# Row loads, row stores and stores of the normed tiles issued from GpSimd's queue in the last mixing stage of a hybrid encoder layer

## The reference

```
h = rms_norm(x, norm1);  p = h @ w_in
y_a = gated unit on 128-position blocks of (u, v)          # group A
o, S = gated_delta_chunked(q, k, v, g, beta, S0, 64)       # group B, a recurrence over the tiles
x = x + concat(y_a, y_b) @ w_o                             # 1024 x 1024
h2 = rms_norm(x, norm2)
x = x + (silu(h2 @ w_gate) * (h2 @ w_up)) @ w_down         # d_ff = 2816
y = rms_norm(x, final_norm)
```

## Time and profile before

| | us |
|---|---|
| median of 3 runs | 2823.54 (2820.58 to 2824.5) |
| the profiled execution | 2825.7 |
| its span | 2824.0 |
| PE busy in the span | 2730.2 (97%) |
| last mixing stage with its drain, about | 900 to 1181 |

### The profile page before, as it was taken

The page is one execution under the profiler, slowest core; times in us unless marked ns, Lnnn a source line. Parts: engine busy times, 40 slices in busy tenths (PEclk is TensorE's granted clock), DMA queues, the critical chain, the costliest instruction groups (busy, mean ns, idle before and its releaser), DMA issues.

```text
span 2824.0 us, 46417 instructions
## 1 busy us (share of the span) xinstructions
PE 2730.2 (97%) x19256; PEld 2415.0 (86%) x19256; DVE 1408.1 (50%) x2303; ACT 986.1 (35%) x1634; POOL 21.6 (1%) x60
## 2 busy tenths in 40 slices
PE   8999999999999998699999999999999999999998
PEld 7877777777777776599999999999999998999998
DVE  4666667767666565534333345333434345344344
ACT  3436556655555554411111214122111134222222
POOL 2000000000000000000000000000000000000000
PEclk9999999999999999899999999999999999999999
DMA  9355444444544856532122225212222152222220
GB/s 298 96 165 175 124 124 150 137 123 124 173 123 124 155 174 226 186 112 60 59 60 74 59 66 192 70 60 59 74 59 59 67 172 75 75 74 74 74 74 37
DMA packets 361901, 315.13 MB, mean 112 GB/s; under 512 B 15653, under 2 KB 315762, under 8 KB 359714
## 3 DMA queue, kind: packets, MB, share of 16 engines
q1 hardware_dynamic: 361762, 313.20, 37.1%
HBM read 254.80 MB, written 58.36 MB: 111 GB/s over the span
## 4 chain that ended last, share of the span: by engine, by line
PE 56%; DVE 1%; ACT 1%; issue 0%; DVEq 0%; POOL 0%; ACTq 0%; POOLq 0%
PE gate_ps L2586 7%; PE gate_ps L2588 7%; PE gate_ps L2587 7%; PE up_ps L2588 6%; PE up_ps L2587 6%; PE up_ps L2586 6%; PE down_ps L2587 6%; PE down_ps L2588 6%; PE down_ps L2586 6%; DVE w_in_sb L2580 0%; ACT h_hi L2382 0%; ACT w_hi L2363 0%; DVE w_in_sb L2481 0%; DVE h_lo L2503 0%; DVE w_in_sb L2525 0%
## 5 line engine op out<-in xcount | busy, mean ns | idle before, releaser
L1640 PE MATMUL pr_p<-hT_hi_p,w_hi_p 128*128 128x512 f32 x992 | 424.9, 428 | 10.9 <-DVE hT_lo_p L1081 8.9
L1641 PE MATMUL pr_p<-hT_lo_p,w_hi_p 128*128 128x512 f32 x992 | 392.9, 396 | 0.0
L1642 PE MATMUL pr_p<-hT_hi_p,w_lo_p 128*128 128x512 f32 x992 | 392.8, 396 | 0.0
L2467 DVE TENSOR_TENSOR w_in_sb<-up_ps,w_in_sb 128x384 f32<-128x384 f32 (+1 forms) x132 | 70.7, 536 | 604.6 <-PE up_ps L2588 604.6
L2586 PE MATMUL gate_ps<-h_hi,w_hi 128*128 128x384 f32 (+1 forms) x1056 | 345.9, 328 | 17.2 <-DVE w_lo L2457 14.4
L2587 PE MATMUL gate_ps<-h_lo,w_hi 128*128 128x384 f32 (+1 forms) x1056 | 345.4, 327 | 0.0
L2588 PE MATMUL gate_ps<-h_hi,w_lo 128*128 128x384 f32 (+1 forms) x1056 | 345.3, 327 | 0.0
L2586 PE MATMUL up_ps<-h_hi,w_hi 128*128 128x384 f32 (+1 forms) x1056 | 344.0, 326 | 0.0
L2587 PE MATMUL up_ps<-h_lo,w_hi 128*128 128x384 f32 (+1 forms) x1056 | 343.9, 326 | 0.0
L2588 PE MATMUL up_ps<-h_hi,w_lo 128*128 128x384 f32 (+1 forms) x1056 | 343.9, 326 | 0.0
L2481 DVE TENSOR_TENSOR w_in_sb<-down_ps,w_in_sb 128x1024 f32<-128x1024 f32 x187 | 228.8, 1223 | 183.1 <-PE down_ps L2588 182.2
(11 more groups left out here) (378 smaller groups left out, 4063.4 us busy)
## 6 DMA issues: line engine op xcount, KB each, us to landing
w_in_sb<-in_w_in SPq DMA_DIRECT2D x100, 512.0 KB, 4.4
w_in_sb<-in_w_gate SPq DMA_DIRECT2D x66, 512.0 KB, 4.0
w_in_sb<-in_w_up SPq DMA_DIRECT2D x66, 512.0 KB, 5.2
w_in_sb<-in_w_down SPq DMA_DIRECT2D x33, 1024.0 KB, 4.9
stream_tiles<-w_in_sb SPq DMA_DIRECT2D x96, 256.0 KB, 2.5
w_in_sb<-stream_tiles SPq DMA_DIRECT2D x16, 1280.0 KB, 7.1
w_in_sb<-mixed_tiles SPq DMA_DIRECT2D x29, 512.0 KB, 5.0
out<-w_in_sb SPq DMA_DIRECT2D x21, 512.0 KB, 4.0
```

Source lines behind the costliest of these rows:

```text
L1640: pe.matmul(out, w_h, x_h, start=start, stop=False)
L1641: pe.matmul(out, w_h, x_l, start=False, stop=False)
L1642: return pe.matmul(out, w_l, x_h, start=False, stop=stop)
L2467: dve.tensor_tensor(act[:, h, 0:half], up_ps[h][:, 0:half], gate_act[:, h, 0:half], ALU.mult)\
```

## The change

The three helpers `load_rows`, `store_rows` and `store_h2` go from SP's list to POOL's, with the waits and semaphores that they had. On SP the calls of them in `quarter` fall away; nothing else of SP's list is touched. On POOL they stand behind the last `memset` in one loop over the items: load of n, both stores of the normed tile n-3, store of n-1. These are 84 transfers of 256 KB (12 loads and 12 stores of first items; 24 loads, 12 stores and 24 stores of normed halves of second items).

```
@@ SP, quarter(n, part)
                 if part == 0:
                     load_weights(n + 3)
                     if n in (ITEMS - NI + 1, ITEMS + 1):
                         load_wo(0 if n < ITEMS else 1)
-                    if ITEMS <= n < ALL:
-                        load_rows(n)
-                if part == 3:
-                    if ITEMS < n <= ALL:
-                        store_rows(n - 1)
-                if part == 2 and ITEMS + DONE + 3 <= n < ALL + 3:
-                    store_h2(1, n - 3)
-                if part == 0 and ITEMS + DONE + 3 <= n < ALL + 3:
-                    store_h2(0, n - 3)
@@ POOL, behind the last memset
+            def load_rows(n):
+                m, ring = nth(n), nth(n) % 2
...
+                else:
+                    pool.wait_ge(half_stored[ring], 16 * (DONE // 2))
+                    if m >= 2:
+                        pool.wait_ge(row_stored[ring], 16 * (m // 2))
+                        pool.wait_ge(s["h_ready"], TILES + m - 1)
...
+                    pool.dma_start(rows_of[ring][:, 0:HC], a["x1"][m][:, 0:HC]).then_inc(row_loaded[ring], 16)
+                    pool.dma_start(rows_of[ring][:, HC:], a["x"][m][:, HC:]).then_inc(row_loaded[ring], 16)
...
+            for n in range(ITEMS, ALL + 3):
+                if n < ALL:
+                    load_rows(n)
+                if n >= ITEMS + DONE + 3:
+                    store_h2(0, n - 3)
+                    store_h2(1, n - 3)
+                if ITEMS < n <= ALL:
+                    store_rows(n - 1)
```

More of the change, by code:

```diff
@@ L447, in load_wo @@
                 sp.dma_start(hraw, wo_dram[:, :, half * HC:(half + 1) * HC]).then_inc(s["wo_loaded"], 16)
[L449 to L481, removed]
             def quarter(n, part):
@@ L696, in _, with store_rows, store_h2 @@
             pool.memset(XT[:], 0.0).then_inc(s["lx_zeroed"], 1)
+            def load_rows(n):
+                m, ring = nth(n), nth(n) % 2
+                if kind(n) == "first":
+                    if m < 2:
+                        pool.wait_ge(plain_stored[ring], stored_by(MACROS - 1, ("z",), "plain", ring))
+                    else:
+                        pool.wait_ge(half_stored[ring], 16 * (m // 2))
+                    pool.dma_start(plain[:, ring], a["x"][m][:, 0:HC]).then_inc(half_loaded[ring], 16)
+                else:
+                    pool.wait_ge(half_stored[ring], 16 * (DONE // 2))
+                    if m >= 2:
+                        pool.wait_ge(row_stored[ring], 16 * (m // 2))
+                        pool.wait_ge(s["h_ready"], TILES + m - 1)
+                    else:
+                        pool.wait_ge(conv_stored[ring], stored_by(MACROS - 1, ("k", "q", "v"), "conv", ring))
+                        pool.wait_ge(conv_stored[1 - ring], stored_by(MACROS - 1, ("k", "q", "v"), "conv", 1 - ring))
+                        pool.wait_ge(s["h_ready"], TILES)
+                    pool.dma_start(rows_of[ring][:, 0:HC], a["x1"][m][:, 0:HC]).then_inc(row_loaded[ring], 16)
+                    pool.dma_start(rows_of[ring][:, HC:], a["x"][m][:, HC:]).then_inc(row_loaded[ring], 16)
+            def store_rows(n):
+                m, ring = nth(n), nth(n) % 2
+                if kind(n) == "first":
+                    pool.wait_ge(s["first_added"], m + 1)
+                    pool.dma_start(a["x1"][m][:, 0:HC], plain[:, ring]).then_inc(half_stored[ring], 16)
+                else:
+                    pool.wait_ge(s["second_added"], m + 1)
+                    pool.dma_start(a["x1"][m][:, HC:], rows_of[ring][:, HC:]).then_inc(row_stored[ring], 16)
+            def store_h2(i, n):
+                m = nth(n)
+                pool.wait_ge(s["h2_ready"], 2 * m + i + 1)
+                pool.dma_start(a["h2t"][m][:, i * HC:(i + 1) * HC], cin[:, i, 0:HC]).then_inc(h2_stored[i], 16)
+            for n in range(ITEMS, ALL + 3):
[6 more added lines that the diff above has]
+                    store_rows(n - 1)
         @block.scalar
```

## The result

The changed kernel takes 2838.28 us (median of 4 runs, 2832.55 to 2841.76) against 2824.02 (4 runs, 2820.58 to 2824.69): ratio 1.0049, 95% interval 1.0036 to 1.0062. It is slower by 0.5%, where 2817.3 was forecast, and it lies above the range of 2808 to 2832.

What follows compares the result with a forecast made beforehand. PE, busy 97% of the span, was taken as the bound, so only its waits could be won: -1.9 - 4.8 + 2.8 - 1.7 - 0.6 = -6.2 us, from 2823.5 to 2817.3, range 2808 to 2832.

Steps and rivals of the forecast that it cites:

- The first items: First items, wait for the weight behind the halo stores: both stay on SP in the same order, so 0 us.
- The clause on POOL's rows that push in between: First items: two 256 KB rows from POOL pushing in beside the halo would cost 3 us; kept for the range only.
- The end: Barrier after the mixing stage: the last normed half lands last, at 1178.4 instead of the mixed tile at 1179.1; -0.6 us.
- Issue time: Price g of one transfer issue on POOL: taken as 1.0 us, between 0.32 and 1.67; a loss from 1.3.
- The cheap rival: Issues on POOL cost 0.53 us, like its memset; lag 4.2, time 2808.5; chance 0.12.
- The lag: Second items, from the end of scaling L1374 to the start of L1146: 5.6 us forecast, 4.9 in ordinary turns before.
- Landing: Second items, time from a normed store's issue until its data have landed: 2.5 us taken, against a median of 4.1.
- Items 3 and 7: Two second items with long lags, 7.5 and 10.4 us, both to fall to 5.6: -1.9 and -4.8 us.
- the ordinary turns: Six other turns of second items: lag 0.7 us longer each, two thirds of it felt by PE; +2.8 us.
- The clock: Stretches of items 3 and 7: the lowered clock cost 5.0 us, a third comes back as PE idles less; -1.7 us.
- Dear issues: Rival: POOL issues cost 1.67 us, lag 7.6, stores of normed halves come later every turn; +8.5 us, 2832; chance 0.25.
- The rival on traffic: Second items: traffic on shared engines, not the queue, held the row stores, so they land as late; 2824; chance 0.18.

Runs made afterwards that it cites:

- e4: The changed kernel with the 12 stores of halo issued one to each item from the seventh on, not in a row: 2869.44 us, 1.0146 against the kernel before.
- e9: The kernel before, all transfers on SP, with both stores of normed halves put ahead of the row loads in each second item: 2815.60 us, 0.9969.
- e10: The kernel with only second items' transfers on POOL, there with stores of normed halves ahead of row loads: 2819.24 us, 0.9977 against the kernel before.
- e2: The kernel before with only the first items' row loads and row stores moved to POOL: 2832.88 us, 1.0029.
- e13: e2 with SP's load of z and streams held until the row load of first item 8 has landed: 2830.70 us, 1.0033 against the kernel before.
- e12: The kernel before plus three unneeded 256 KB loads from POOL's queue beside the stores of halo, SP's list untouched: 2828.44 us, 1.0018.

## Why the prediction was wrong

- **The first items: term 0, measured +4.9 to +7.3 by the first mark, +5.1 to +5.7 from the third add on.** This is the step that failed first. "Weight and halo both stay on SP, in the same order" is true and not enough. Before, SP's one queue kept the issues apart: a row store went out behind the 12 stores, and the streams behind the row load. On POOL's queue the rows are under way together with the halo, and SP, freed of them, issues the streams ahead of the row load. DVE then stood 13.3 us for that load instead of 7.4, and the weight came 3.2 us later. The clause on POOL's rows that push in between named the first of this and priced it at 3 us, as 512 KB at the normal rate; beside stores with 4 bytes to a run one row store took 19 to 23 us (13 behind them). That SP would issue streams sooner the prediction saw too, but only for the second items.

  The Trainium skill, "DMA: Bandwidth & Descriptors", SWDGE vs HWDGE vs iDMA, says that transfers issued by GpSimd and by SP feed different queues inside each DMA engine, which takes them in turn. The runs fit this: with POOL's loads beside them the 12 issues went from 9.99 to 16.25 us, and a load of 256 KB took 13, where the normed halves, as large, land in 2.3 to 7.3. The taking in turn itself no run shows.

- **The end: term -0.6, measured +3.2 to +3.5.** The last half did land when it should (issue over at 1179.2, SP's waits done at 1181.2). But I asked only when the data are there, not what POOL itself has to do before it arrives at the barrier. Its DRAIN was not in any row of before, since POOL had no transfers.

- **Issue time: taken as 1.0, measured 0.54.** The cheap rival's value, POOL's memset, was right. By that rival's sum the kernel should have taken 2808.5. What the sum took as 0.1, the time from the end of the scaling to POOL's issue, is 0.6 (SP 0.1).

- **The lag: forecast 5.6; measured 5.7 in item 3, 6.7 in item 7, 6.5 in the mean of the other seven turns from the second to the tenth (before 5.3).** Landing was mis-sized: 2.5 taken, 4.5 in item 7 and 4.1 in the median. The reason I gave, that with 1 us between issues the two row loads are mostly gone, fell with the issue time: at 0.54 they are just ahead. Items 3 and 7 gave 1.8 and 3.7 of lag, near the 1.9 and 4.8 I had; the ordinary turns cost 1.2 each, seven of them, 8.2. One of them, 5.4 grown to 8.5 us, is the turn beside which the four loads now come, which was named and given no price. From first to last scaling the change is then -1.5 in one profile and +2.0 in the other, where the sum had -5.6. Kernels with second items as before take 116.5 to 118.7 us there, kernels with those of the change (e4 aside) 116.9 to 120.4: nothing.

- **The clock: term -1.7.** The granted clock did rise, 0.83 to 1.00 between 1060 and 1080 and 0.85 to 1.00 between 1100 and 1120, more than the third that the sum took, but the idle time of PE between 1060 and 1160 went from 13.5 to 14.6 us (100 less 85.45) where 10 was forecast. PE was idle where it had been full, which the prediction itself had named as a sign of being wrong.

- **The rivals.** Dear issues gave a time that is near (2832), for a reason that is not there. The rival on traffic, 2824, had the size right for the second items and not the reason: row stores did not land as late on POOL's queue (waits of 4.1 us instead of 17.5), but the ordinary turns took the gain back. e9 and e10, the same order on SP and on POOL, take 108.9 and 109.9 us, so the queue itself gives them nothing. That is what the Trainium skill, "DMA: Bandwidth & Descriptors", Issuing engines are not separate DMA queues, had said, that only issue time is saved. None of the rivals held the two places outside the second items, where the loss arose.

- **What I did not see.** The loop of the second items was read rightly (scaling, row loads, halves, L1146), and e9 shows that its lag was worth 9.5 us. But the prediction kept the order as given and asked only which queue it should stand on.

What stays open: how the 8 us of e2 divide between the stretched halo, the row store caught in it and the streams ahead of the row load (e13's median gives the streams almost nothing, its trace two thirds), and why single runs of these kernels lie 5 to 10 us apart.

## What to carry to other kernels

Before moving transfers to a second queue, list what the one queue kept apart by its order: here small-run stores beside 256 KB rows cost more than the issue time saved, and they are found in stages the change was not meant for. Ask of a wait in a queue which of the transfers behind it need it; putting those that don't ahead of it (e9) brought 9 us where the second queue brought none. And price the end of a phase for every engine that gets new work, not only for the data.

## What the runs showed of the hardware that I had not expected

- POOL's issue of a transfer took 0.54 us for 256 KB (128 rows) and 0.52 us for 32 bytes (31.26 us for 60). Behind a wait for DVE's scaling it began 0.6 us after the scaling's end, SP's 0.1 us.
- POOL's DRAIN at the barrier took 3.3, 3.8, 5.5, 7.5 and 10.4 us with 24, 36, 60, 84 and 120 transfers issued from its queue in the phase, and 0.31 at most with three, all waited for (the row of e12):

```profile
L183 POOLq DRAIN  x3: 40/290/311, 994.4 to 1178.8; - x3
```

- The 12 stores of halo, 18 KB in all, cost the kernel before 6.9 us (2818.70 against 2825.58), and 7.7 in the traces from the third add to the first scaling (105.7 less 98.0), and in the changed kernel twelve single ones cost 31 us more than twelve in a row.
